# First head staged in the projection, carried squares added on GpSimd, the even layer's statistics in the modulation, and earlier fetches: eight-part network on one core

## The reference

```python
for i in range(4):                       # the first network
    kind, j = i % 3, i // 3
    if kind == 0: x = x + _diff_attention(_rms_norm(x, a_norm_g[j]), ...)  # 8 heads x 2 maps, causal by chunks
    elif kind == 1: x = x + _conformer_conv(_rms_norm(x, b_norm_g[j]), ...)
    else: x = x + _mla(_rms_norm(x, c_norm_g[j]), ...)                     # 8 heads, causal by chunks
# each mixer ends with (o * silu(gate)) @ w_out

# the second network, layer by layer (0 is even, 1 is odd)
sh1, sc1, g1, sh2, sc2, g2 = split(silu(cond) @ w_mod + b_mod, 6)          # for latent and for context
h = rmsnorm(x, norm1_g) * (1 + sc1) + sh1
if even:
    u, v = split(gelu(h @ w_in[:, :2 * 1024]))
    y_a = u * (w_s applied to layernorm(v) along the tokens, + b_s)         # gMLP
    vb, x1, x2 = split(short_conv(h @ w_in[:, 2 * 1024:]))
    z = x2 * long_conv(x1 * long_conv(vb, filter0), filter1)                # Hyena, by DFT
    x = x + g1 * (concat(y_a, z) @ w_out)
else:
    x = x + g1 * (gqa(rmsnorm(q), rmsnorm(k), v) @ w_o)                      # 8 heads on 2 key heads
x = x + g2 * swiglu(rmsnorm(x, norm2_g) * (1 + sc2) + sh2)
```

## Time and profile before

| | |
|---|---|
| time, median of 3 runs | 3787.21 us (3784.91 to 3788.84) |
| the profiled execution | 3787.38 us; its span 3785.6 us |
| granted TensorE clock, mean | 0.947 |
| PE busy | 3336.8 us, 88% |
| PEld, DVE, ACT, POOL busy | 69%, 48%, 32%, 2% |
| DMA | 292 MB, 77 GB/s on average |

### The profile page before, as it was taken

The page is one execution under the profiler, slowest core; times in us unless marked ns, Lnnn a source line. Parts: engine busy times, 40 slices in busy tenths (PEclk is TensorE's granted clock), DMA queues, the critical chain, the costliest instruction groups (busy, mean ns, idle before and its releaser), DMA issues. The chain is left out here.

```text
span 3785.6 us, 41142 instructions
## 1 busy us (share of the span) xinstructions
PE 3336.8 (88%) x16280; PEld 2623.5 (69%) x16280; DVE 1831.5 (48%) x2739; ACT 1221.4 (32%) x2115; POOL 58.1 (2%) x69
## 2 busy tenths in 40 slices
PE   7987997988898779776979989789999988989998
PEld 5865665656687544576868856668888867767876
DVE  4545597443463746673243459542222245443333
ACT  3245323345332612463211212232121233632221
POOL 0000000000000000000000002100000000000000
PEclk9998999998999889898989999899999999999998
DMA  3222111201222211692011122111111111122221
GB/s 139 82 55 69 67 56 47 75 30 60 75 80 62 73 60 78 233 355 78 23 67 67 45 77 78 67 45 56 67 66 56 56 64 28 37 78 90 99 89 56
DMA packets 49235, 292.00 MB, mean 77 GB/s; under 512 B 7495, under 2 KB 7751, under 8 KB 17912
## 3 DMA queue, kind: packets, MB, share of 16 engines
q1 hardware_dynamic: 47032, 283.05, 21.2%
q0 software_dynamic: 2048, 6.82, 0.6%
HBM read 262.84 MB, written 14.68 MB: 73 GB/s over the span
## 5 line engine op out<-in xcount | busy, mean ns | idle before, releaser
L407 PE MATMUL bank<-high,slot_high 128*128 128x512 f32 (+1 forms) x3344 | 1241.0, 371 | 126.7 <-DVE low L331 96.7
L408 PE MATMUL bank<-low,slot_high 128*128 128x512 f32 (+1 forms) x3344 | 1225.0, 366 | 0.0
L409 PE MATMUL bank<-high,slot_low 128*128 128x512 f32 (+1 forms) x3344 | 1222.0, 365 | 0.0
L387 DVE TENSOR_TENSOR slot_low<-slot,slot_high 128x2048 fp32r<-128x2048 f32 (+1 forms) x172 | 389.9, 2267 | 1220.0 <-ACT slot_high L381 1219.7
L407 PEld LDWEIGHTS bank<-high,slot_high 128*128 128x128 f32 x3344 | 633.4, 189 | 262.9 <-issue 126.1
L381 ACT ACTIVATE slot_high<-slot 128x2048 fp32r<-128x2048 f32 (+1 forms) x172 | 325.7, 1894 | 1376.8 <-PE bank L409 1161.3
L408 PEld LDWEIGHTS bank<-low,slot_high 128*128 128x128 f32 x3344 | 634.6, 190 | 112.2 <-issue 6.5
L409 PEld LDWEIGHTS bank<-high,slot_low 128*128 128x128 f32 x3344 | 633.6, 189 | 110.2
L877 DVE TENSOR_REDUCE peak<-bank 128x1 f32<-128x128 f32 (+2 forms) x224 | 109.5, 507 | 173.9 <-PE bank L1002 74.4
L929 ACT ACTIVATE prob<-bank,peak_bias 128x128 f32<-128x128 f32 (+2 forms) x224 | 119.8, 540 | 109.9 <-DVE peak_bias L885 109.6
L444 PE MATMUL bank<-slot_high,high 128*128 128x256 f32 x448 | 127.0, 283 | 27.3 <-DVE low L329 27.3
(11 more groups left out here) (376 smaller groups left out, 4053.3 us busy)
## 6 DMA issues: line engine op xcount, KB each, us to landing
mod_raw<-in_mod SPq DMA_DIRECT2D x48, 1024.0 KB, 7.3
slot<-in_gu SPq DMA_DIRECT2D x44, 1024.0 KB, 4.8
slot<-in_a_in SPq DMA_DIRECT2D x32, 1024.0 KB, 4.8
slot<-in_e_rest SPq DMA_DIRECT2D x16, 1024.0 KB, 4.8
slot<-in_down SPq DMA_DIRECT2D x16, 1024.0 KB, 4.8
spectra<-f_spectrum SPq DMA_DIRECT2D x12, 1024.0 KB, 3.9
h_spectrum<-spectra SPq DMA_DIRECT2D x12, 1024.0 KB, 5.0
slot<-in_a_out SPq DMA_DIRECT2D x8, 1024.0 KB, 6.2
```

The source lines that it names most:

```text
L387: dve.tensor_tensor(k.slot_low[s][:, 0:n], k.slot[s][:, 0:n], k.slot_high[s][:, 0:n].bitcast(F32), ALU.subtract).then_inc(k.low[s], 1)
L407: pe.matmul(out, wh, xh, start=kt == 0, stop=False)
L408: pe.matmul(out, wh, xl, start=False, stop=False)
L409: mm = pe.matmul(out, wl, xh, start=False, stop=kt == self.kt - 1)
```

## The change

Six edits, all in the order or the place of work.

1. The copies for head 0 (and its masks) are issued in the projection's block, by SP after its last weight fetch and a wait for `heads_scaled` (DVE raises it when the tiles of head 0 are final), by POOL at that block's beginning (in `project_q` after `heads_scaled`). The attention's block begins with head 1. `q_now0` and `k_now0` are allocated around both blocks.
2. In attention the output projection's first two slots are fetched behind the staging of head (2, 1) instead of (3, 1); ACT makes their high halves at blocks 24 and 26, DVE their low halves at 26 and 28.
3. `TailSquares`: GpSimd adds the squares of tiles 0 to 5 to `square_sum`, and PE has three products after the last slot (the sum, tiles 6 and 7) where it had eight, four of them between the slots.
4. The statistics of the even layer's first norm run in `modulation`: squares and their sum before the first piece on ACT and PE, the mean on DVE and the root on ACT behind the first four pieces, the reciprocal on DVE behind the last. `gmlp` takes them as `given`. Its first pair of slots (now e_rest, pair 0) is fetched at the modulation's end, its order is gates[0], val, gates[1], and the first slot is multiplied tile by tile as the tiles become ready.
5. `gmlp` fetches and halves the first slots of `project_half` with e_out0 as its `follow`.
6. In `long_conv` PE waits for the DFT table behind the first transposes and no more ahead of them.

```diff
@@ class SplitNorm
     def scalar(self, k, act, u):
-        for y, (kt, r) in enumerate([] if self.summed else self.order):
...
-        halve_first(k, act, u, "take_high", self.phase, 0)
-        for r, (c, n) in enumerate(self.ranges):
...
+        if not (self.summed or self.given):
+            self.square(k, act)
+        halve_first(k, act, u, "take_high", self.phase, 0)
+        if not self.given:
+            self.take_roots(k, act, u)
         halve_first(k, act, u, "take_high", self.phase, 1)
         self.feed.scalar(k, act)
...
+        if not self.given:
+            self.take_means(k, dve, u)
+        halve_first(k, dve, u, "take_low", self.phase, 0)
+        if not self.given:
+            self.invert(k, dve)
+        if not (self.summed or self.given):
+            halve_first(k, dve, u, "take_low", self.phase, 1)
+        self.feed.vector(k, dve)
+        if self.summed or self.given:
+            halve_first(k, dve, u, "take_low", self.phase, 1)
@@ class TailSquares
                 if f >= 4:
-                    act.wait_ge(self.added.sem, self.added.at(f - 3))
+                    act.wait_ge(self.added.sem, self.added.at(max(f - 4, 1)))
...
+    def pool(self, pool):
+        for f in range(1, 6):
+            pool.wait_ge(self.squared.sem, self.squared.at(f + 1))
+            if f > 1:
+                pool.wait_ge(self.added.sem, self.added.at(f - 1))
+            pool.tensor_tensor(self.sum[:, :], self.ring[0][:, 0:LAT] if f == 1 else self.sum[:, :],
+                               self.ring[f % 4][:, 0:LAT], ALU.add).then_inc(self.added.sem, 1)
@@ class Attention
-    HALVES_AT = 27, 29
+    HIGHS_AT, LOWS_AT = (24, 26), (26, 28)
...
     def stage_heads(self, k, engine, u):
...
             for hh in range(2):
+                if (i, hh) == (0, 0):
+                    continue
                 if i:
                     engine.wait_ge(k.filled[b], u.full(b, i * 4 + (2 * hh - 3)))
...
+                stage_head(k, engine, self.stage, i, hh)
+                if (i, hh) == (2, 1):
+                    self.follow.fetch(k, engine, u)
@@ project_a, sync (project_up and project_q alike)
+            heads = k.named("heads_scaled")
+            sp.wait_ge(heads.sem, heads.at(2))
+            stage_head(k, sp, stage, 0, 0)
@@ project_a, gpsimd
+            fill_masks(k, pool, masks, 0)
@@ modulation
+            first.fetch(k, sp, u[0])
...
+            stats.square(k, act)
+            turn(0)
+            stats.take_roots(k, act, u[1])
             loop(act, turns, turn, first=1)
...
+            stats.tensor(k, pe, u[2].copy())
             pe.wait_ge(halved.sem, halved.at(2))
...
+            turn(0)
+            stats.take_means(k, dve, u[3])
+            loop(dve, turns, turn, first=1)
+            stats.invert(k, dve)
             dve.wait_ge(k.filled[2], u[3].full(2))
@@ gmlp
+    gates = [first, SplitPairs(w["e_rest"], 2, 1, ranges=BOTH)]
+    norm = modulated_split(k, op, mod, gain, 0, 0, BOTH, first, given=True)
...
-            low = k.named("tile_low")
-            pe.wait_ge(low.sem, low.at(2 * KT))
+            gates[0].multiply(k, pe, u[1], op.moving(BOTH), norm.ready(k, pe))
             val.multiply_tokens(k, pe, u[1], lambda kt, tt: op.tile(kt, tt * P, P))
-            gate.multiply(k, pe, u[1], op.moving(BOTH))
+            gates[1].multiply(k, pe, u[1], op.moving(BOTH))
...
+            follow.fetch(k, sp, u[0])
@@ long_conv, tensor
-            pe.wait_ge(loaded.sem, loaded.at(32))
...
+                if e == 0:
+                    pe.wait_ge(loaded.sem, loaded.at(32))
```

More of the change, by code:

```diff
@@ L1006, in stage_a @@
                                 lambda kt, i, hh: cols(V, i * 256 + (kt * D + hh * P), P), True, O, neg_lam, ssq,
-                                masks=masks, transfers=8, follow=out)
+                                masks=[masks(h) for h in range(2)], transfers=8, follow=out)
                 attend(k, att)
@@ L1671, in _ @@
             low = k.named("tile_low")
-            behind, last = tail.tensor(pe, u[1])
-            out.multiply(k, pe, u[1], op.moving(LATENT), lambda kt: pe.wait_ge(low.sem, low.at(kt + 1)), behind)
-            last()
+            out.multiply(k, pe, u[1], op.moving(LATENT), lambda kt: pe.wait_ge(low.sem, low.at(kt + 1)))
+            tail.tensor(pe, u[1])
             u[1].add([7])
+        @block.gpsimd
+        def _(pool):
+            tail.pool(pool)
         def make(kt, dst):
@@ L1962, in _ @@
             pool.dma_start(spread_in, w["spread_c"]).then_inc(table_in.sem, 16)
+            fill_masks(k, pool, masks, 0)
+        @block.sync
+        def _(sp):
+            heads = k.named("heads_scaled")
+            sp.wait_ge(heads.sem, heads.at(1))
+            stage_head(k, sp, stage, 0, 0)
             close(u[0])
@@ L3133, in even_layer @@
                     op.ring = [k.sb(f"whole{x}", BANK, ring)[:, :] for x in range(4)]
-                    gmlp(k, w, mod, gain, z, op)
+                    gmlp(k, w, mod, gain, z, op, first, half)
                 with ExitStack() as ring:
-                    project_half(k, w["e_out0"], tile_of(z),
+                    project_half(k, half, tile_of(z),
                                  Operand(k, ring, TOK, ring=False), scale, middle)
@@ L3439, in scale @@
                 ins.then_inc(k.drained[b], 1)
+                if n in (1, 2):
+                    for bank, use in ((0, 2), (1, 1)) if n == 1 else ((b, use),):
+                        dve.wait_ge(k.drained[bank], x.full(bank, use))
+                    dve.sem_inc(heads.sem, 1)
             def finish(x, m):
```

259 lines of the change are left out of this document (143 added, 116 removed).

## The result

| | before | changed |
|---|---|---|
| median | 3786.06 us (4 runs, 3781.53 to 3788.84) | 3684.11 us (4 runs, 3676.50 to 3689.55) |
| ratio, 95% interval | | 0.973 (0.9709 to 0.9752) |
| span of the profiled run | 3785.6 us | 3687.8 us |
| granted clock, mean | 0.947 | 0.959 |

The kernel is 102 us faster; 3694 was forecast. The changed kernel, run again beside later experiments (e11), had 0.9726 (0.971 to 0.9741).

The account below looks back on a forecast made before the run. PE, busy 88% of the span, was taken as the bound, except in the DMA-bound modulation. Savings of 33.9, 16.6, 17.8, 13.2, 7.2 and 4.6 sum to 93.3, taking 3787.4 to 3694 us, range 3676 to 3715.

Parts of the forecast that it names:

- The starts: Heads of the four attention blocks: PE's gaps shrink and its clock behind them stays higher; 33.9 us saved.
- rival (e): A copy or fetch is held by a wait behind which nothing moves; 3750 us at worst, chance 3 in 100.
- The ends: Ends of the four attentions: earlier halvings cut PE's waits on mix; 16.6 us saved, 6.5 in each diff attention.
- 5.6 of 12.4 stay: Ends of the diff attentions: of 12.4 us lost in each, halvings still cost 5.6, so 6.5 is gained.
- The tails: Four output-projection tails: GpSimd's adds relieve PE of products, 4.4 us each; 17.8 us saved.
- 4p − 20: Tails: PE's wait in us per tail if a GpSimd add takes p us; late from about 6 us per add.
- The modulation and gmlp: Statistics moved into the modulation: gmlp's start gains 23.7 us, the modulation pays 10.5; net 13.2 us saved.
- Rival (a): The DMA-bound modulation pays for what gmlp wins, that term becoming +1; 3709 us, chance 15 in 100.
- project_half: Block with e_out0: its first slot already there and halved shortens the wait before the first matmul; 7.2 us saved.
- long_conv: Block's head: the first transposes and their copy go into the wait for the DFT table; 4.6 us saved.
- Rival (b): Attention's starts and ends only move their wait, head 1 late by 2.5 us; 3708 to 3714 us, chance 15 in 100.
- rival (c): More is won than counted, above all at attentions' ends and by clock after the starts; 3670 us, chance 12 in 100.

Follow-up runs that it names:

- e11: The changed kernel itself, unedited, run once more as the base for the runs beside it; 3680.38 us, ratio 0.9726 to the kernel before.
- e1: The changed kernel with part 1 undone: copies and masks of heads 0 and 1 issued in the attention's block again; ratio 0.9813 to the kernel before.
- e2: The changed kernel with part 2 undone: slots fetched behind head (3, 1), both engines halving at blocks 27 and 29; ratio 0.9794 to the kernel before.
- e7: The changed kernel with DVE's low halves in attention at blocks 24 and 26, the same as ACT's high halves; ratio 0.9801 to the kernel before.
- e3: The changed kernel with part 3 undone: PE adds all eight squares in each tail; ratio 0.9763 to the kernel before.
- e9: The changed kernel with three extra unread GpSimd adds ahead of each of the five in a tail; one run, 3711.73 us.
- e10: The changed kernel with seven extra unread GpSimd adds ahead of each of the five in a tail; one run, 3806.74 us.
- e4: The changed kernel with the first norm's statistics back in gmlp, its new slot order and early fetch kept; ratio 0.9745 to the kernel before.
- e6: The changed kernel with GpSimd squaring X beside the modulation's pieces, PE adding between them, roots and reciprocals later; 3674.11 us, ratio 0.9713 to the kernel before.

## Why the prediction was right, point by point

1. **The starts**, 33.9 forecast: 36 by stretches, 31 by time (e1). The gaps went by 8.8, 8.9, 3.9 and 5.1, each within half a microsecond of its term. The clock behind them gave 9.4 where I had 6.8. The 0.6 for a late head 1 was not needed, and the copies do not hold the end of the projection's block: PE's work from its first slot on takes 194.0 to 194.1 us before and after, in both diff attentions, so rival (e) did not come. (As worked there, the two diff attentions come to 9.7 and 10.7, where 9.9 and 10.8 were added; it changes nothing.)
2. **The ends**, 16.6 forecast: 24 to 25 (e2). This is the term that was mis-sized. The step that failed is "each halving still pushes the chain by 1 to 2 us: 5.6 of 12.4 stay". Some 2.5 stay. I had read the low half's 2.3 us against DVE's 1.3 us of slack in a group; but e7, with the same halvings in the same stretch and DVE waiting 3.5 and 3.8 for ACT, loses 9 to 10 us, more than the two waits together. The loss was the wait with peaks and mixes queued behind it, for which PE waits, and PE's clock, 0.66 there instead of 0.80; the 2.3 us themselves are mostly taken up within the next blocks. The texts ahead of the result also have the move wrong: ACT's high halves went ahead by three blocks each (27 to 24, 29 to 26), but DVE's low halves by one (27 to 26, 29 to 28), so that the change is above all a separation. And the sum slips: the two waits are 12.8 us, not 12.4, and 12.4 less 5.6 is 6.8, where 6.5 was taken.
3. **The tails**, 17.8 forecast: 17.1 by stretches (e3), the time saying 10 to 14. An add took 1.29, below the 1.8 of the earlier trace rows. The bound "late from about 6 us", and 4p − 20 with it, was too generous: e9 and e10 fit 4p − 16.6, with the chain's start at 361.1 and the need at 377.7, so the sum is late from about 4.2 us an add. It changed nothing at 1.29.
4. **The modulation and gmlp**, 13.2 forecast: from the filters' last matmul to gmlp's mixing 332.7 us before and 315.8 after, 16.9. The modulation's own price, 10.5 forecast, was 8.5 in this pair of profiles (from the filters' last matmul to the product with its finished rows 150.6 and 159.1): the 7.5 us hole of the DMA engines was forecast at 6.5 (5.8 by the times given there), the root's 2.5 came as 0.9, and the reciprocals end 1.3 behind PE's last product, where 1.5 was taken. The size is less sure than the sum of its parts: the modulation's length in like profiles spreads from 154.2 to 163.1, mean 158.2, against 151.6 in the one profile of the kernel before. gmlp's first product came 10.5 us behind the modulation's last, and the following slots 4.3 us slower (140.86 to 145.13), 23.7 forecast for both and 25.5 measured. The statistics alone are worth 7 to 8.5 of it (e4). In e4 the same stretch is 322.6, so 10.2 of the 16.9 are there without them; they go to the new order of the slots with its early fetch and its product tile by tile, which no run takes apart. Rival (a) did not come.
5. **project_half**, 7.2 forecast: 7.2. **long_conv**, 4.6 forecast: 4.4.

Rival (b) did not come: head 1 is in time, and the halvings won more than their term. What came goes the way of rival (c), above all at the attentions' ends, where it named them: 3684 lies 10 below the forecast and 14 above its 3670. That the total fell so near the forecast owes nothing to terms that cancel; all that missed by more than 1 us (1, 2 and 4) were too small by the stretches.

Terms by stretches add up to 107, against 102 measured and 97.8 between the two profiles. The difference lies in stages that the change does not touch, feed_forward 0 foremost, 7.1 us longer in the changed kernel's profile.

What stays open: why feed_forward 0 has two durations, why the modulation's length spreads by 9 us among like profiles, and whether part 3 is worth its 17 us by stretches or the 10 to 14 of the times; the intervals of two ratios, 6 to 8 us each way, allow either.

## What to carry to other kernels

Where one engine's work is made of another's (here a low half out of a high half), give the second engine its turn some blocks after the first's, even if both are then late (in the diff attentions that cost nothing, in MLA 2.5 us); the wait costs more than itself, since all that stands behind it on an in-order engine waits too. What opens a block (copies, masks, first slots) could be issued in the block before at no cost that these stretches show, and the clock that PE keeps is part of the gain; statistics moved the same way did cost, since ACT was needed at that block's head. In a stage that is bound by its transfers ask of each instruction put at the head whether it stands between a landing and the buffer's release: on an idle engine, as GpSimd in e6, they left no hole.

## What the runs showed of the hardware that was not expected

The same 3168 matmul records of feed_forward 0 took 562.4 us in one run of the changed kernel (e11) and 569.4 in another, with clocks of 1.00 and 0.99. Windows over them, e11 and then the first profile:

```profile
2416.30:2978.70 562.40, 557.19 (x3168) 487.21 (x3169) 155.75 (x195) 115.04 (x141) 0.32 (x1) 1.00 0.17 59
```

```profile
2417.30:2986.70 569.40, 564.63 (x3168) 490.44 (x3168) 155.74 (x195) 114.93 (x141) 0.29 (x1) 0.99 0.17 58
```

Five of the nine profiles in the table have 561.9 to 563.2, four 568.2 to 569.5, variants of the changed kernel in both; DVE's and ACT's busy times are the same, so it is PE that is 1.2% slower, and throughout: in windows of 100 us, all at a clock of 1.00, it has 567 to 569 matmuls against 574 to 576 in the kernel before. It is not the chip either: of four kernels run on one chip, e1 and e3 have the short time and e2 and e4 the long one. It is as much as one of the smaller parts of the change is worth, and was found only by reading the same stretch in many profiles.

"SBUF — State Buffer" of the Trainium skill (section on the two separate sides) has a GpSimd instruction and a DVE instruction with two SBUF inputs hold one port pair in turn, each for its whole length; e9, e10 and e6 agree, with 3.35 us for an add of 1.26 and up to 3.33 for a low half of 2.29, and the tails of the changed kernel, where they seldom meet, show 1.29 and 2.29.
